# Four buffers for gathered token rows instead of two, and the gather issued two pairs earlier

## The reference

```python
grp_onehot = one_hot(argmax(xt @ moe_w_group + b), 4)          # one of 4 groups
top_val, top_idx = top_k(logits within that group, 2)          # 2 of its 8 experts
combine = grp_onehot[:, :, None] * within[:, None, :]          # weight per token and expert
for g in range(4):
    a = einsum('nd,edf->nef', xt, moe_w_gate[g])               # 1024 -> 256
    b = einsum('nd,edf->nef', xt, moe_w_up[g])
    act = silu(a) * b * combine[:, g, :, None]
    out += einsum('nef,efd->nd', act, moe_w_down[g])           # 256 -> 1024
x = x + gate2 * out
```

## Time and profile before

| what | us |
|---|---|
| median of 3 runs | 957.45 (955.76 to 958.22) |
| profiled execution, its own time | 955.04 |
| span in the profile, first to last instruction | 953.3 |
| TensorE matmul busy in the span | 724.4 (76%) |
| VectorE, ScalarE, GpSimd busy | 352.5, 204.6, 74.6 |
| mean granted TensorE clock | 0.858 |
| DMA issues of the experts' weights | 64 of gate, 64 of up (512 KB each), 32 of down (1024 KB each) |

### The profile page before, as it was taken

How to read it: one execution, slowest core, us unless ns; L and a number is a source line. 1 busy time by engine, 2 the same in 40 slices (tenths; PEclk the granted TensorE clock), 3 DMA queues, 4 the chain that set the end, 5 groups by cost and what they waited for, 6 DMA issues and landing times.

```text
span 953.3 us, 8400 instructions
## 1 busy us (share of the span) xinstructions
PE 724.4 (76%) x3154; PEld 376.2 (39%) x3154; DVE 352.5 (37%) x892; ACT 204.6 (21%) x440; POOL 74.6 (8%) x128
## 2 busy tenths in 40 slices
PE   4489999957668997998599995695777757886900
PEld 2155665546453342775354433432322223232300
DVE  2293755645533235345425536211101111101167
ACT  2421314243433445111020102010101001100111
POOL 4001002020100001000010000100001100010000
PEclk9789999987758998699699998598788987889855
DMA  9941110042220125931397116379998999999662
GB/s 289 380 181 40 48 56 33 1 176 89 89 89 6 60 116 204 324 127 64 105 378 240 44 45 227 92 262 370 363 348 321 371 347 361 348 354 369 233 208 99
DMA packets 53474, 187.31 MB, mean 196 GB/s; under 512 B 7915, under 2 KB 12891, under 8 KB 45718
## 3 DMA queue, kind: packets, MB, share of 16 engines
q1 hardware_dynamic: 36614, 156.82, 43.8%
q10 hardware_dynamic: 11040, 18.73, 6.0%
q0 software_dynamic: 5776, 11.19, 3.7%
HBM read 176.83 MB, written 17.21 MB: 204 GB/s over the span
## 4 chain that ended last, share of the span: by engine, by line
PE 57%; DMA 17%; DVE 14%; ACT 5%; issue 4%; POOL 1%; ACTq 1%; SPq 0%; POOLq 0%; DVEq 0%
PE ps L1508 52%; DMA sb<-h_rows,sb 14%; DVE sb L915 9%; PE ps L1575 4%; DMA sb<-in_x_sample 1%; ACT sb L698 1%; POOL y_rows L542 1%; DVE sb L1485 1%; DMA sb<-in_ssm_b_im 1%; DVE sb L1501 1%; ACT sb L617 1%; DMA sb<-y_rows 1%; DMA out_hgrn_sample<-sb 1%; DVE sb L1211 0%; PE ps L1672 0%
## 5 line engine op out<-in xcount | busy, mean ns | idle before, releaser
L1508 PE MATMUL ps<-sb 128*64 128x512 f32 (+9 forms) x2738 | 657.8, 511 | 76.2 <-DVE sb L915 24.9
L1508 PEld LDWEIGHTS ps<-sb 128*128 128x128 f32 (+4 forms) x2738 | 318.3, 173 | 381.1 <-issue 328.9
L915 DVE TENSOR_TENSOR sb<-sb 128x16 f32<-128x16 f32 (+17 forms) x367 | 166.8, 497 | 113.9 <-ACT sb L698 58.1
L1575 PE MATMUL ps<-sb 128*128 128x128 f32 (+1 forms) x208 | 42.0, 369 | 77.9 <-DMA sb<-h_rows,sb 73.7
L915 DVE TENSOR_TENSOR sb<-ps,sb 128x256 f32<-128x256 f32 (+6 forms) x69 | 28.9, 440 | 156.5 <-ACT sb L867 118.0
L1575 PEld LDWEIGHTS ps<-sb 128*128 128x128 f32 (+1 forms) x208 | 35.1, 210 | 96.6 <-DMA sb<-h_rows,sb 85.2
L1485 DVE TENSOR_SCALAR sb<-ps,sb 128x512 f32<-128x512 f32 x16 | 12.0, 751 | 74.0 <-PE ps L1508 74.0
L1465 DVE COPY sb<-ps 128x512 f32<-128x512 f32 x16 | 11.0, 690 | 71.9 <-PE ps L1575 71.9
L542 POOL DMA_INDIRECT y_rows<-sb x16 | 16.3, 1019 | 260.6 <-DVE sb L1485 250.3
L698 ACT COPY sb<-ps 32x144 f32<-32x144 f32 x64 | 26.3, 412 | 34.6 <-PE ps L1508 33.2
L863 ACT COPY sb<-ps 128x512 f32<-128x512 f32 x16 | 9.4, 586 | 111.3 <-PE ps L1575 111.3
(11 more groups left out here) (226 smaller groups left out, 326.9 us busy)
## 6 DMA issues: line engine op xcount, KB each, us to landing
sb<-in_moe_w_gate SPq DMA_DIRECT2D x64, 512.0 KB, 12.1
sb<-in_moe_w_up SPq DMA_DIRECT2D x64, 512.0 KB, 13.2
sb<-in_moe_w_down SPq DMA_DIRECT2D x32, 1024.0 KB, 7.6
sb<-in_w_ada SPq DMA_DIRECT2D x12, 2048.0 KB, 7.8
sb<-in_w_in SPq DMA_DIRECT2D x5, 2048.0 KB, 18.3
sb<-in_w_ada_final SPq DMA_DIRECT2D x4, 2048.0 KB, 15.2
sb<-in_w_out SPq DMA_DIRECT2D x2, 2048.0 KB, 7.7
sb<-in_x_prompt SPq DMA_DIRECT2D x4, 512.0 KB, 10.3
```

The lines of the kernel that those rows point to most:

```text
L915: return dve.tensor_tensor(out, x0, x1, op)
L1508: return pe.matmul(out, lhsT, rhs, start=start, stop=stop, skip_group_check=True)
L1575: ins = pe.transpose(banks[c // 4][:, P * (c % 4):P * (c % 4) + r], src[0:r, c:D:KC], ident[0:r, 0:r])
```

## The change

There are four buffers `xg`, with a semaphore each. The two new ones lie in the region of `h2T`, behind the two result buffers `yb`; the routed branch does not read `h2T` after the router's logits. GpSimd issues the gathers of pairs 0 to 3 at the start, and in iteration p the gather of pair p+4, still in front of the scatter of pair p and still behind the wait for `turn(p)`. TensorE's `turn` waits for the semaphore of the buffer it reads. Nothing else in the order of any engine is changed. As two more semaphores are needed, three that belonged to the final normalisation (`x3_sq`, `x3_ms`, `x3_rt`) are dropped, and their instructions count on in three older ones (`ssq`, `ms`, `rms`).

```diff
-        xg = [at(XG + D * k, D) for k in range(2)]
+        xg = [at(off, D) for off in (XG, XG + D, MIXT + 2 * D, MIXT + 3 * D)]
+        DEEP = len(xg)
...
                 def gather(n_):
-                    pool.indirect_dma_start(out=xg[n_ % 2], out_offset=None, in_=h2_dram,
+                    pool.indirect_dma_start(out=xg[n_ % DEEP], out_offset=None, in_=h2_dram,
                                             in_offset=at_rows(gidx[:, n_:n_ + 1]), bounds_check=NT - 1,
-                                            oob_is_err=False).then_inc(S[f"xg{n_ % 2}"], 16)
+                                            oob_is_err=False).then_inc(S[f"xg{n_ % DEEP}"], 16)
 
                 pool.wait_ge(S["tabs"], 1)
-                gather(0)
-                gather(1)
+                for n_ in range(DEEP):
+                    gather(n_)
                 pool.wait_ge(S["tabs"], 2)
                 for p_ in range(PAIRS):
-                    if p_ + 2 < PAIRS:
+                    if p_ + DEEP < PAIRS:
                         pool.wait_ge(S["xt_mm"], 2 * p_ + 2)
-                        gather(p_ + 2)
+                        gather(p_ + DEEP)
...
                 act.activation(acc[0:r, t, :], x[0:r, t, :], ACT.Square, accum_out=ss[0:r, t:t + 1])\
-                   .then_inc(S["x3_sq"], 1)
-            act.wait_ge(S["x3_ms"], 1)
-            act.activation(rs[:, 0:TILES], ss[:, 0:TILES], ACT.Sqrt).then_inc(S["x3_rt"], 1)
+                   .then_inc(S["ssq"], 1)
+            act.wait_ge(S["ms"], 2)
+            act.activation(rs[:, 0:TILES], ss[:, 0:TILES], ACT.Sqrt).then_inc(S["rms"], 1)
...
                 def turn(n_):
 
-                    pe.wait_ge(S[f"xg{n_ % 2}"], 16 * (n_ // 2 + 1))
+                    pe.wait_ge(S[f"xg{n_ % DEEP}"], 16 * (n_ // DEEP + 1))
                     if n_ >= 1:
                         pe.wait_ge(S["xt_dve"], n_)
                         pe.wait_ge(S["xt_act"], n_)
-                    turn_tile(0, xg[n_ % 2], (ps[0], ps[1]), S["xt_mm"])
+                    turn_tile(0, xg[n_ % DEEP], (ps[0], ps[1]), S["xt_mm"])
```

More of the change, by code:

```diff
@@ L296, in decoder_step @@
             "lg_mm", "rt_exp", "rt_exp2", "acc_zero",
-            "gu_mm", "g_sig", "act_ready", "at_mm", "at_out", "y_mm", "y_acc", "gs_mul", "flag", "pos", "hot", "tab_mm", "tabs", "gu_half", "lg_read", "rank_mm", "SM_ready", "before", "xg0", "xg1", "xt_mm", "xt_act", "xt_dve", "ys0", "ys1", "yb_act", "yb_dve", "comb2", "xg_init",
-            "x3", "x3_sq", "x3_ms", "x3_rt", "y_ready", "written")}
+            "gu_mm", "g_sig", "act_ready", "at_mm", "at_out", "y_mm", "y_acc", "gs_mul", "flag", "pos", "hot", "tab_mm", "tabs", "gu_half", "lg_read", "rank_mm", "SM_ready", "before", "xg0", "xg1", "xt_mm", "xt_act", "xt_dve", "xg2", "xg3", "ys0", "ys1", "yb_act", "yb_dve", "comb2", "xg_init",
+            "x3", "y_ready", "written")}
         def used_up(n):
@@ L1492, in _ @@
                     gate2(t)
-            dve.wait_ge(S["x3_sq"], TILES)
-            dve.tensor_scalar(ss[:, 0:TILES], ss[:, 0:TILES], 1.0 / D, EPS, ALU.mult, ALU.add).then_inc(S["x3_ms"], 1)
-            dve.wait_ge(S["x3_rt"], 1)
+            dve.wait_ge(S["ssq"], 2 * TILES)
+            dve.tensor_scalar(ss[:, 0:TILES], ss[:, 0:TILES], 1.0 / D, EPS, ALU.mult, ALU.add).then_inc(S["ms"], 1)
+            dve.wait_ge(S["rms"], 2)
             link(dve.reciprocal(rs[:, 0:TILES], rs[:, 0:TILES]))
```

## The result

The changed kernel takes **924.3 us** (922.92 to 927.85), beside 957.84 for the kernel before in the same comparison (955.76 to 959.8): a ratio of 0.966, 95% interval 0.964 to 0.9681. The forecast was 935 with a range of 927 to 948: the direction and the next bound came as forecast, but the gain was 33.5 us instead of 22, outside the range.

What follows compares the result with a forecast made beforehand. TensorE waits for gathers, with DMA nearly full behind it. Thirteen bursts 19.7 + tail 3.1 - start 0.5 = 22.3 us off 955.04 gives 932.7; with 2.4 for the runs' median, 935, range 927 to 948.

Steps and rivals of the forecast that it cites:

- 1, gather wait: Routed-expert stage, TensorE: the wait of `turn` for gathered rows goes, removing 5.2 us a pair.
- 2, next bound: Routed-expert stage: gate/up waits for weights; SyncE issues 8.4 us behind a landing, so DMA never runs dry and bounds.
- 3, DMA period: DMA time per expert pair: 17.9 us (17.5 to 18.4) instead of 19.50, saving 1.6 us a pair.
- 4, the thirteenth burst's landing: End of the stage's thirteen weight bursts: last landing at 869.4 instead of about 889.1, 19.7 us earlier.
- 5, tail: From the last weights' landing to the last scaling: 13.5 us instead of 16.6, 3.1 us saved.
- 6, start: Start of the gathers: four go out instead of two, so the first may land later; 0.5 us lost.
- 7, semaphores: Merged semaphores at the kernel's end: same instructions wait for the same events, no cost.
- the dips: DMA running dry between weight bursts, laid to SyncE issuing later weights only behind `down`; 0.36 busy from 773 to 777 us.
- Rival D: Stage DMA: gathers and scatters cost only their bytes, all at 419 GB/s, 16.5 us a pair; 915 us, chance 0.05.
- Rival B: TensorE in the stage: new waits lower its clock, 24.3 us a pair, 62 us lost; 1019 us, chance 0.03.
- Rival A: Stage DMA gives no more than now, period about 19.3 us, gain 5 us; 952 us, chance 0.09.
- Rival C: GpSimd's queue still holds gathers back behind the scatter, so TensorE still waits; 955 to 957 us, chance 0.03.

Runs made afterwards that it cites:

- run 9: Kernel before with only the merged semaphores of the final normalisation: 956.69 us against 956.63, ratio 1.0006.
- run 2: Changed kernel, but SyncE holds each burst of weights until the last piece of the burst before has landed: 968.17 us, ratio 1.0147 to the kernel before.
- run 4: Changed kernel with SyncE's order turned, gate and up pieces of pair n+1 ahead of the down piece of pair n: 913.89 us, ratio 0.9569.
- run 3: Changed kernel with the wait for the previous burst's landing in every second burst only: 940.9 us, ratio 0.9836.
- runs 7 and 8: Changed kernel without the gathers of pairs 4 to 15: 913.11 us; changed kernel without the scatters of pairs 2 to 15: 908.56 us.
- Run 5: Kernel before, gathers as they were, with only SyncE's order turned (gate and up pieces ahead of the down piece): 949.98 us, ratio 0.9952.
- run 1: Kernel before with its two buffers, only GpSimd's order changed so that gathers go out earlier, ahead of the scatter: 925.42 us, ratio 0.970.

## Why the prediction was wrong

By its own steps, in the profiled executions (955.04 before, 922.92 after: 32.1 us, forecast 22.3):

| step | forecast | measured |
|---|---|---|
| 1, gather wait | gone | gone beyond the first |
| 2, next bound | the weights, DMA never dry | so; next burst 8.37 us behind a landing in the pair shown (8.4) |
| 3, DMA period | 17.9 (17.5 to 18.4) | 17.06 |
| 4, the thirteenth burst's landing | 869.4, 19.7 us earlier | 861.9, 27.2 us earlier (the start's 0.4 within) |
| 5, tail | 13.5, 3.1 us shorter | 11.9, 4.7 us shorter |
| 6, start | 0.5 us later | first scaling 636.99 against 636.56: 0.4 later |
| 7, semaphores | nothing | nothing (run 9) |

**The step that failed is 3, the DMA period**, as the prediction put it: "I take 17.9, between the two, with 17.5 and 18.4 as ends". The next bound was the one foretold (step 2); its size, this term of the sum, was 0.8 us a pair too long. Its error carries the 7.5 us by which step 4 is off: from 637.0 + 1.7 to 861.9 the thirteen bursts took 17.2 us each. Both ways to that number, the busy share (0.927 × 19.50 = 18.1) and the mixed rate (372 GB/s), took rows of bursts that had started on a queue run dry or nearly so, as if busy time were the work that remains. Run 2 shows that it is not: gathers early, nothing else changed, but each burst dry, and DMA's busy time is back at 18.1 us a pair and the weights at 2.65 us per MB. With a queue that never ran dry the same bytes took 2.51, so part of the "busy" share was the price of starting dry, and it went when the dips went. Another part is how the share reads: with the queue full it was 1.02 over 187.7 us, so a period of 17.06 us holds 17.4 us of busy time. Of the 1.0 us between 18.1 and 17.06, 0.7 is busy time that went and 0.3 is this reading. Rival D pointed that way, and gave its price too far: 16.5 us a pair at 419 GB/s; the stage runs at 406. The result lies midway between the forecast's 935 and D's 915, which the prediction had given a chance of 0.05.

What in a dry burst makes DMA slow is not settled, but where it is slow can be read. Cut into windows of 1 us, the middle of the stage has 18 with DMA at least 0.9 busy and under 350 GB/s in the kernel before (of 159 so busy), 21 of 157 in run 2, 7 of 187 in the changed kernel, 0 of 182 in run 4. In run 2 all but one of the 21 begin 7 to 10 us behind the first issue of a burst, in every one of its ten bursts; in run 3 there are 10 of 170, all so placed, and only behind bursts that were held back. So the price is not paid at the start of a burst alone. As an estimate, with the changed kernel's rate as what the bytes are worth (1.02 of busy share at 406 GB/s), each burst of run 2 has some 0.4 us of busy time too much in its first two microseconds and 0.8 from 7 to 10 us behind its issue. The slow microseconds are not made by the gathers or the scatters alone: runs 7 and 8, without the one or the other, still have 3 and 7, while run 4 has both and none.

**A reason that was wrong beside the number.** The prediction laid the dips of DMA to SyncE's order, down pieces first. Run 5 turned that order and the dips stayed. In the kernel before it was the loop through the gather that made everything late, 19.3 us long by the rows; DMA ran dry as a consequence. The order costs something only once that loop is gone (run 4).

**The tail** was 1.6 us shorter than taken because the clock did not fall (1.00 from 861.91 to 873.79): the second half of gate/up, both `down`s and the transposes took 11.9 us, the 12.05 of the full clock, without the allowance for the low one. Rival B was wrong in its sign: with waits of 3.5 us at most instead of 4.4 to 6.6, the mean granted clock of the stage went up, 0.85 to 0.95, and `turn` took 1.16 instead of 1.97.

**Rival A** is refuted: 406 GB/s over 188 us. The Trainium skill ("DMA: Bandwidth & Descriptors", Specifications) states an HBM limit of about 358 GB/s for a core, and the trace does not agree with that row read alone. The Trainium skill elsewhere ("Perfetto Trace Analysis", Roofline) calls 358 GB/s the share of a core when both of a pair are active, and takes some 120% of it as the ceiling of one core alone. With that the trace agrees: 406 is 113%. The prediction had weighed the one without the other.

**Rival C** is refuted by the missing wait. But the change's outward form, more buffers, was not its cause (run 1).

## What to carry to other kernels

When a transfer arrives late, look first at what stands ahead of it in the queue that issues it: here a gather whose buffer was free stood behind a scatter that waited for the end of the pair, and moving it needed no memory. When a stall in front of a transfer queue is removed, price the new bound from bytes and from stretches far from any dip; a busy share measured over bursts that start dry contains the price of starting dry. Here the 419 GB/s of such a stretch would have given 16.5 us, 3% too short, where the 17.9 taken was 5% too long. Once the queue is full, look at its start: closing the hole ahead of the first full burst, with the fuller queue that came of it, brought about 9 us more (ratio 0.966 to 0.9569).

## What the runs showed that had not been expected

DMA's busy share is not a measure of work: 2.65 us per MB of weights with each burst dry, 2.62 before, 2.56 with every second burst dry, 2.51 after, 2.47 with the order of run 4. Holding each burst back until the one before had landed lengthened the period by 3.8 us, from 17.06 to 20.90, 2.8 us of it idle and the rest slower transfer; that is more than the whole gain of the change (19.50 to 17.06). And an issue of SyncE can itself take long: 3.31 us for one with the queue full, where the median of the stage is 0.48.
